# Matmuls of a feed-forward product regrouped by width, one wait split in two, and the order of three engines' work near the end

## The reference

```python
def conv_ffn(h, up, conv_w, conv_b, down):
    hid = causal_dwconv(h @ up.astype(h.dtype), conv_w, conv_b)
    gate, val = jnp.split(hid, 2, axis=-1)
    return (jax.nn.gelu(gate) * val) @ down.astype(h.dtype)
...
    y = conv_ffn(h, ffn_up[l], ...)
    x = x + rms_norm(y, post_ffn_norm[l])
```

## Time and profile before

| | |
|---|---|
| median of 3 runs | 2677.85 us |
| profiled execution | 2677.78 us |
| its span | 2676.0 us |
| PE busy | 2648.5 us, 99% |
| DVE busy | 1893.4 us, 71% |
| ACT busy | 1111.9 us, 42% |
| POOL busy | 306.3 us, 11% |

### The profile page before, as it was taken

One profiled execution on the slowest core, in us unless ns is written; L12 is line 12 of the kernel. 1 busy time (PEld: TensorE's weight loads), 2 busy tenths in 40 slices (PEclk: granted clock), 3 DMA queues, 4 the chain that ended last, 5 costly groups with the idle time before them and its releaser, 6 DMA issues.

```text
span 2676.0 us, 36733 instructions
## 1 busy us (share of the span) xinstructions
PE 2648.5 (99%) x15008; PEld 2205.4 (82%) x15008; DVE 1893.4 (71%) x2456; ACT 1111.9 (42%) x1442; POOL 306.3 (11%) x324
## 2 busy tenths in 40 slices
PE   9999999999999999999989999999999999999998
PEld 8778877877888888788868888888888888888888
DVE  6557467773554665623988788888888888888885
ACT  5335255632422333422653444344444444444444
POOL 1003100350000000011010011111110111111014
PEclk9999999999999999999999999999999999999999
DMA  6225412452232211233375577777777777777674
GB/s 231 87 87 196 126 64 66 155 183 91 85 110 88 100 65 66 97 124 110 134 134 159 149 166 172 172 150 166 152 173 164 165 152 166 168 172 169 142 207 171
DMA packets 297940, 370.38 MB, mean 138 GB/s; under 512 B 10016, under 2 KB 264096, under 8 KB 279216
## 3 DMA queue, kind: packets, MB, share of 16 engines
q1 hardware_dynamic: 231712, 260.23, 30.1%
q0 software_dynamic: 65776, 107.56, 20.8%
q10 hardware_dynamic: 288, 0.27, 0.0%
HBM read 297.77 MB, written 62.91 MB: 135 GB/s over the span
## 4 chain that ended last, share of the span: by engine, by line
PE 94%; DVE 2%; DMA 2%; ACT 1%; issue 1%; POOL 0%; DVEq 0%; ACTq 0%; POOLq 0%
PE ps L1681 16%; PE ps L972 10%; PE ps L974 10%; PE ps L973 10%; PE ps L1682 8%; PE ps L1731 5%; PE ps L1733 5%; PE ps L1732 5%; PE ps L1685 2%; PE ps L1581 1%; PE ps L1580 1%; PE ps L1579 1%; PE ps L1684 1%; PE ps L1138 1%; PE ps L1139 1%; PE ps L1140 1%
## 5 line engine op out<-in xcount | busy, mean ns | idle before, releaser
L2423 ACT ACTIVATE w_hi<-raw 128x1024 fp32r<-128x1024 f32 x360 | 381.2, 1060 | 601.7 <-PE ps L1685 222.5
L3505 DVE TENSOR_TENSOR w_lo<-raw,w_hi 128x1024 fp32r<-128x1024 f32 x360 | 439.9, 1222 | 128.0 <-ACT w_hi L2423 121.1
L972 PE MATMUL ps<-h_both,w_hi 128*128 128x512 f32 x1200 | 481.5, 401 | 0.0
L974 PE MATMUL ps<-h_both,w_lo 128*128 128x512 f32 x1200 | 468.1, 390 | 0.0
L973 PE MATMUL ps<-h_both,w_hi 128*128 128x512 f32 x1200 | 467.7, 390 | 0.0
L1681 PE MATMUL ps<-h_both,w_hi 128*128 128x512 f32 x1120 | 401.7, 398 | 3.6 <-DVE w_lo L3505 3.6
L2572 DVE TENSOR_TENSOR w_lo<-raw,w_hi 128x2048 fp32r<-128x2048 f32 x103 | 241.7, 2346 | 199.8 <-ACT w_hi L1839 199.6
L1839 ACT ACTIVATE w_hi<-raw 128x2048 fp32r<-128x2048 f32 x103 | 196.8, 1911 | 353.2 <-PE ps L974 310.1
L1682 PE MATMUL ps<-h_both,w_lo 128*128 128x256 f32 x1120 | 314.2, 281 | 0.0
L972 PEld LDWEIGHTS ps<-h_both,w_hi 128*128 128x128 f32 x1200 | 225.3, 188 | 57.5 <-issue 11.1
L974 PEld LDWEIGHTS ps<-h_both,w_lo 128*128 128x128 f32 x1200 | 225.2, 188 | 48.1
(11 more groups left out here) (521 smaller groups left out, 4464.6 us busy)
## 6 DMA issues: line engine op xcount, KB each, us to landing
raw<-weights SPq DMA_DIRECT2D x241, 512.0 KB, 4.8
raw<-weights SPq DMA_DIRECT2D x111, 1024.0 KB, 4.9
y_sum<-y_part POOLq DMA_DIRECT2D x80, 512.0 KB, 5.4
raw<-weights POOLq DMA_DIRECT2D x40, 512.0 KB, 6.2
x_spill<-X POOLq DMA_DIRECT2D x8, 1024.0 KB, 8.8
x_res<-x_in SPq DMA_DIRECT2D x4, 1024.0 KB, 6.9
x<-X POOLq DMA_DIRECT2D x4, 1024.0 KB, 4.5
x_res<-x SPq DMA_DIRECT2D x4, 1024.0 KB, 7.0
```

Source lines behind the costliest of these rows:

```text
L972: pe.matmul(o, w_hi[:, s % 2, w], h_hi[:, t, :], start=(t == 0), stop=False)
L974: mm = pe.matmul(o, w_lo[:, s % 2, w], h_hi[:, t, :], start=False, stop=(t == 15))
L2423: A(hi_form(f), raw_block(p), ACT.Copy).then_inc(w_hi_ready, 1)
L3505: V.tensor_tensor(lo_form(f), raw_block(p), hi_form(f).bitcast(F32), ALU.subtract).then_inc(w_ready, 1)
```

## The change

In `product` the seven wide matmuls of steps 0 to 6 run first, then the eight narrow ones, then the wide one of step 7. The wait on the low weights moves from the start to just before the narrow ones, and a wait on the high weights stands at the start. In POOL's order the squares of tiles 1 and 2 come before `load_y(3)`, and two more squares come before each `x_back` load; the remaining three follow. In ACT's order `step_hi_end(2)` moves ahead of the square of tile 2 and `step_hi_end(3)` ahead of that of tile 5.

```diff
             store_y(HALVES - 2)
             store_y(HALVES - 1)
+            add_squares(6, range(3), TOK_1)
             load_y(3)
             for k in range(4):
+                add_squares(6, range(3 + 2 * k, 5 + 2 * k), TOK_1)
                 pool.dma_start(x_back(4 * k, 4), x_spill2[:, 4 * k:4 * k + 4, :]).then_inc(sem("x_back"), 16)
-            add_squares(6, range(14), TOK_1)
+            add_squares(6, range(11, 14), TOK_1)
...
             def product(f, bank, both, high=0):
+                o, o_low = ps[:, bank, :], ps[:, bank, 256 * high:256 * high + 256]
+                cols = [form_cols(f, 128 * k) for k in range(8)]
+                pe.wait_ge(w_hi_ready, hi_ready(f))
+                for k in range(7):
+                    half, w = cols[k]
+                    pe.matmul(o, w_hi[:, half, w], both[:, k, :, :], start=(k == 0), stop=False)
                 pe.wait_ge(w_ready, ready(f))
                 for k in range(8):
-                    half, w = form_cols(f, 128 * k)
-                    o, o_low = ps[:, bank, :], ps[:, bank, 256 * high:256 * high + 256]
-                    if k < 7:
-                        pe.matmul(o, w_hi[:, half, w], both[:, k, :, :], start=(k == 0), stop=False)
-                        pe.matmul(o_low, w_lo[:, half, w], both[:, k, high, :], start=False, stop=False)
-                    else:
-                        pe.matmul(o_low, w_lo[:, half, w], both[:, k, high, :], start=False, stop=False)
-                        pe.matmul(o, w_hi[:, half, w], both[:, k, :, :], start=False, stop=True).then_inc(w_used, 1)
+                    half, w = cols[k]
+                    pe.matmul(o_low, w_lo[:, half, w], both[:, k, high, :], start=False, stop=False)
+                half, w = cols[7]
+                pe.matmul(o, w_hi[:, half, w], both[:, 7, :, :], start=False, stop=True).then_inc(w_used, 1)
...
-                    if n in (3, 7):
+                    if n in (2, 5):
                         step_hi_end(n // 4 + 2)
```

## The result

The changed kernel took 2661.27 us (median of 4 runs, 2660.99 to 2662.51), the kernel before 2678.72 us beside it (4 runs): ratio 0.9933, 95% interval 0.992 to 0.9945, 17.5 us less. The prediction was 2660, range 2651 to 2670.

What follows compares the result with a forecast made beforehand. The prediction took PE, busy 99% of the span, to bound the kernel: 2677.78 us less 9.3 (products), 1.3 (last stall) and 7.7 (end) gave 2659.5, predicted as 2660 us, range for 8 in 10 2651 to 2670.

Steps and rivals of the forecast that it cites:

- Cost of a product: PE's products: regrouping takes each from 2.820 to 2.785 us, saving 0.035 us over 267 products, 9.3 us.
- The narrow group: Eight narrow matmuls in a product: the first at 0.113 us, the other seven at 0.120 us each.
- the wide one: Wide matmuls in a product: six at 0.227 us, the first of the group and the closing one at 0.235 us.
- The 2.820: Time in us of a product before the change, from six whole products in 16.92 us.
- Rival (a): Products on PE: order does not matter, only the stall terms are gained, 2668.8 us; chance 0.20.
- rival (d): Products on PE: eight narrow matmuls into the same columns stand 0.15 us apart, 56 us slower, 2716 us; chance 0.05.
- The last stall among the products: PE's stall ending at 1414.92 us: the product then ends 1.3 us earlier, bounds 0 and 1.6.
- the head start of the wide group: At that last stall, the wide group needs only the high part and the take, starting at 1413.65 us; gain 1.3 us.
- the waits would move to the first narrow matmul: Sign among the products: the 14.2 us of waits leave the wide line for the narrow one and stay above 10.
- The end: Near 2619 to 2628 us: PE's 6.13 us stall and 1.53 us of slow clock go, 7.7 us, bounds 4 and 8.
- The chain of causes: At the end: POOL's squares behind the loads delay ACT's square, then the third unit's rounding, DVE's subtraction and PE, 6.13 us.
- Sum: Whole kernel: 2677.78 - 9.3 - 1.3 - 7.7 = 2659.5 us; against the median 2659.6.

Runs made afterwards that it cites:

- product alone: The kernel before with only `product` regrouped, with its two waits; POOL's and ACT's orders at the end as before: 2670.45 us, ratio 0.9968.
- end alone: The kernel before with only POOL's and ACT's new orders at the end, `product` as before: 2670.46 us, ratio 0.997.
- rounding alone: The kernel before with only ACT's `step_hi_end` moved ahead of tiles 2 and 5: 2672.85 us, ratio 0.9973.
- squares alone: The kernel before with only POOL's order changed, ACT's roundings still ahead of tiles 3 and 7: 2670.59 us, ratio 0.9965.
- groups of two: The changed kernel with the product in alternating groups of two wide and two narrow matmuls, and one wait at the start: 2667.74 us.
- two groups: The changed kernel with one wait and the product as four wide, four narrow, three wide, four narrow, closing wide: 2664.11 us.
- one wait in the changed kernel: The changed kernel, but with the low weights waited for ahead of the wide group, as before the change: 2662.59 us.

## Why the prediction was right, point by point

**Cost of a product.** Forecast 2.785 us and 0.035 saved, 9.3 us in all; measured 2.793 (two products in a row) and 0.0285 saved, 7.6 us. The narrow group was right: 0.113 + 7 x 0.120 = 0.953, measured 0.953 on average. The mis-sized term is the wide one: I had one slow wide matmul at the head of the group and 0.227 behind it, but seven take 1.607 us behind a closing wide one and 1.587 behind a down half. On average over the 228 products that follow a product, the seven distances are 0.236, 0.228, 0.233, 0.231 and three times 0.227 us, so the slowness lasts over four matmuls; behind a down half all seven are 0.227. The 2.820 was also taken for every product, where the 38 behind a down half took 2.812 before. The forecast treated them alike, but the 228 gained 0.027 us each and the 38 gained 0.040. Rival (a), no effect of order, is refuted by the product alone and by the two kernels with smaller groups. The Trainium skill ("TensorE: Matmul & The Clock Gate", section "Back-to-back issue gap") gives its formula, columns / 2.4 plus 2.5 ns, for the isolated gap of one matmul. It has no term for the neighbour, but it does not claim that order never matters; that was my reading. In this case a wide matmul in a uniform row takes 227 ns, not the formula's 216, and order is worth 0.0285 us per product. The slower rival (d) did not come: eight narrow ones into one bank half stand 0.119 apart. What about the order matters is only partly shown. It is not the change between high and low weights as such: the down halves change between `w_hi` and `w_lo` too, at one width, and keep 0.227. But narrow matmuls also write half of the bank where wide ones write all of it, and no run separates the width from that.

**The last stall among the products.** Forecast 1.3 us for the head start of the wide group. To leave out the scatter of where DVE stands, I measure from the start of DVE's low part (1413.56 in the earlier trace rows, 1413.15 in the changed kernel) to the closing matmul of the 14th product, in the same way in each trace:

| | granted clock 1.00 | slow clock behind the stall |
|---|---|---|
| one wait | 6.77 to 6.85 us (before, end alone, rounding alone, squares alone, groups of two, two groups) | 8.35 us (one wait in the changed kernel) |
| two waits | 5.61 us (product alone) | 7.15 and 7.16 us (changed kernel, twice) |

The head start is worth 1.2 us in either column, so the mechanism (the wide group starts at the take and not at the low part) and nearly its size were right. What failed is the silent term that the clock stays up: the slow clock cost 1.5 us in either row, more than the head start gives. It fell there in all three profiles of kernels that have the wide matmuls in one group and the new end, and in none of the other seven that have this stall. The forecast that the waits would move to the first narrow matmul was wrong: the takes that `ffn_pair` waits for stand behind the same DVE work, so PE stands there already, and only 0.6 us of the 14.2 appear at the narrow group.

**The end.** Forecast 7.7 us, measured 7.7 in the changed kernel and 7.7 alone. The chain of causes was right too: POOL's additions behind the loads hold up ACT's square, and the rounding stands behind that square. Changing POOL's order alone removed the stall, and with it the slow clock (1.00 instead of 0.51). Breaking the chain one step later, at ACT's rounding, removed the third unit's stall as well and left 1.2 us of waiting for the fourth.

**Sum.** 2659.5 forecast, 2662.5 in the profiled execution, 2661.3 median. The 3.0 us in the profiled one are 1.7 from the wide matmuls and 1.3 from the last stall, whose gain the slow clock took back. Against the kernel before beside it, the gain was 17.5 us where 18.3 were forecast. That the median is nearer than the profile I put down to executions without the slow clock; single runs have no clock by stretch, and both kept profiles of the changed kernel have the slow clock, so this is argued and not shown. That the median came as near as 1.3 us is in part luck, since the scatter of the kernels' medians from set to set is as large.

## What to carry to other kernels

Read a matmul's cost from start to start in a stretch of one shape, and compare it with the stretch that mixes shapes: here the alternating order cost 1% of a product, and groups of four or more got most of it back. When a stall goes, look for its length and for the clock behind it, since 6.1 us of standing cost 7.7. Where an engine's written order puts a short addition behind a load that waits for a store, ask who is queued behind the addition.

## What the runs showed of the hardware that was not expected

Behind a standstill of about 2 us of PE at 1411 to 1413 us, the granted clock fell in some executions (0.63 and 0.74 in the windows above) and stayed at 1.00 in others (kernel before, product alone). The length of this standstill does not decide it alone: the clock fell behind 1.97, 2.05 and 2.17 us, and stayed up behind 2.00 us twice (kernel before, ACT's rounding alone) and behind five shorter ones. All of them had a standstill of 5 us ahead of 1401 to 1403 us as well; what decides is open. Two kernels that differ little can so differ by 1.5 us in one execution.

And the wide matmuls behind narrow ones are slow not once but several times in a row: the first four behind a closing wide one stand 0.236, 0.228, 0.233 and 0.231 us apart, the next three 0.227. No run here says what part of PE causes it.
